# Hybrid decoder trunk (SSD and S5): S5 output and feed-through matrices without their zeros, as 64x64 matmuls on the array's diagonal

## The reference

```python
bu_re = einsum('blgc,gnc->blgn', ug, bbar_re)   # and bu_im
s = associative_scan over l of  s[l] = a * s[l-1] + bu[l]     (complex)
y = einsum('blgn,gcn->blgc', s_re, c_re) - einsum('blgn,gcn->blgc', s_im, c_im)
y = y.reshape(bsz, L, 2048) + d_skip * u
v = gelu(y) @ w_glu
```

## Time and profile before

| | |
|---|---|
| median of 3 runs | 2636.06 us (2634.53 to 2640.14) |
| the profiled execution, its own time | 2637.47 us |
| its span, first to last instruction | 2635.7 us |
| mean granted clock of TensorE | 0.983 |
| PE busy | 2527.9 us (96%) |
| DVE busy | 1684.8 us (64%) |
| ACT busy | 1114.4 us (42%) |

### The profile page before, as it was taken

One profiled execution on the slowest core, in us unless ns is written; L12 is line 12 of the kernel. 1 busy time (PEld: TensorE's weight loads), 2 busy tenths in 40 slices (PEclk: granted clock), 3 DMA queues, 4 the chain that ended last, 5 costly groups with the idle time before them and its releaser, 6 DMA issues.

```text
span 2635.7 us, 53075 instructions
## 1 busy us (share of the span) xinstructions
PE 2527.9 (96%) x19434; PEld 2457.4 (93%) x19434; DVE 1684.8 (64%) x3144; ACT 1114.4 (42%) x1761; POOL 67.4 (3%) x81
## 2 busy tenths in 40 slices
PE   5999999999999999999999999979999999999996
PEld 4989999999999989999999999969999999999996
DVE  4768778786887867668886666574544554544444
ACT  4544535444453534454425333343333443333332
POOL 1000000000000001100000000000000000000000
PEclk9999999999999999999999999989999999999998
DMA  5665657666565668544456776555555555565552
GB/s 149 181 188 171 189 156 213 181 183 191 171 183 170 211 155 232 158 119 135 151 156 199 199 202 188 168 157 165 169 166 163 166 159 166 167 199 166 166 164 73
DMA packets 656789, 450.96 MB, mean 171 GB/s; under 512 B 71160, under 2 KB 647944, under 8 KB 655648
## 3 DMA queue, kind: packets, MB, share of 16 engines
q1 hardware_dynamic: 636480, 433.44, 55.9%
q10 hardware_dynamic: 20128, 15.15, 1.9%
HBM read 409.35 MB, written 39.12 MB: 170 GB/s over the span
## 4 chain that ended last, share of the span: by engine, by line
PE 85%; DVE 9%; issue 3%; ACT 1%; DMA 1%; SPq 0%; ACTq 0%; DVEq 0%
PE acc L1924 26%; PE acc L1925 25%; PE acc L1926 25%; PE side L1911 2%; DVE abc L1322 2%; DVE w_lo L1243 2%; PE side L2241 1%; PE side L2007 1%; PE side L2090 1%; ACT w_hi L773 1%; PE side L2276 1%; PE side L2277 1%; DVE cacc L1286 1%; PE side L2261 1%; PE side L2080 1%
## 5 line engine op out<-in xcount | busy, mean ns | idle before, releaser
L1243 DVE TENSOR_TENSOR w_lo<-raw,w_hi 128x1024 fp32r<-128x1024 f32 (+2 forms) x692 | 846.2, 1228 | 709.3 <-ACT w_hi L773 704.1
L773 ACT ACTIVATE w_hi<-raw 128x1024 fp32r<-128x1024 f32 (+2 forms) x692 | 721.6, 1046 | 1061.8 <-PE acc L1926 1022.8
L1924 PE MATMUL acc<-h_hi,w_hi 128*128 128x288 f32 x3472 | 1056.1, 304 | 14.4 <-DVE w_lo L1243 7.8
L1926 PE MATMUL acc<-h_hi,w_lo 128*128 128x288 f32 x3472 | 1029.8, 297 | 0.0
L1925 PE MATMUL acc<-h_lo,w_hi 128*128 128x288 f32 x3472 | 1028.8, 296 | 0.0
L1924 PEld LDWEIGHTS acc<-h_hi,w_hi 128*128 128x128 f32 x3472 | 659.2, 190 | 33.2 <-issue 24.2
L1925 PEld LDWEIGHTS acc<-h_lo,w_hi 128*128 128x128 f32 x3472 | 658.8, 190 | 0.3
L1926 PEld LDWEIGHTS acc<-h_hi,w_lo 128*128 128x128 f32 x3472 | 657.8, 189 | 0.0
L1924 PE MATMUL acc<-f_hi,w_hi 128*128 128x288 f32 x704 | 208.7, 296 | 0.0
L1926 PE MATMUL acc<-f_hi,w_lo 128*128 128x288 f32 x704 | 207.5, 295 | 0.0
L1925 PE MATMUL acc<-f_lo,w_hi 128*128 128x288 f32 x704 | 207.2, 294 | 0.0
(11 more groups left out here) (345 smaller groups left out, 2898.4 us busy)
## 6 DMA issues: line engine op xcount, KB each, us to landing
raw<-in_w_in_dram SPq DMA_DIRECT2D x512, 256.0 KB, 3.2
raw<-in_w_ffn_up_dram SPq DMA_DIRECT2D x352, 256.0 KB, 3.3
raw<-in_w_ffn_down_dram SPq DMA_DIRECT2D x160, 256.0 KB, 3.0
raw<-in_w_ssm_out_dram SPq DMA_DIRECT2D x128, 256.0 KB, 3.3
raw<-in_w_glu_dram SPq DMA_DIRECT2D x128, 256.0 KB, 3.6
h<-in_state_ssm_dram SPq DMA_DIRECT2D x64, 256.0 KB, 4.2
out_ssm_sample_dram<-h SPq DMA_DIRECT2D x64, 256.0 KB, 2.9
raw<-in_w_out_dram SPq DMA_DIRECT2D x64, 256.0 KB, 3.0
```

What stands on the lines that cost most here:

```text
L773: copy = lambda out, in_, **k: nc.scalar.activation(out, in_, ACT.Copy, **k)
L1243: tt(w_lo[:, slot, 0:n], raw[:, slot, 0:n], w_hi[:, slot, 0:n].bitcast(F32), ALU.subtract).then_inc(lo_ready, 1)
L1924: mm(o_, wh, xh[:, kt, :], start=first and i == 0, stop=False)
L1926: done = mm(o_, wl, xh[:, kt, :], start=False, stop=last and i == n - 1)
```

## The change

The output matrices go into four buffers `obd`, each [128, 2, 8, 64]: the two 64x64 blocks of a pair lie one in the upper and one in the lower 64 partitions, without zeros. They take the memory of `qbd` and `qbd2`. `tbd` is laid out likewise, and its memset goes. Each product becomes two matmuls, one of partitions 0 to 63 into PSUM partitions 0 to 63, one of 64 to 127 into 64 to 127. `o_matrices` and `t_block` write all 128 partitions at once. With four buffers the matrices of blocks 1 to 3 are made at z = 36, 39, 42, 45, 48 and 51, inside the scan, and blocks 4 to 7 after `y_add(i - 4)`.

```diff
-    'tbd_zero': ('dec_raw', 1), 'bbar_ready': ('a_exp', 1), 'u2_landed': ('x_landed', 48),
+    'bbar_ready': ('a_exp', 1), 'u2_landed': ('x_landed', 48),
-    tbd, _ = sb("tbd", [P, 2, PB, P], F32, used["pw5"][0])
+    obd = [sb(f"obd{i}", [P, 2, PB, 64], F32, used["qbd"][0] + 4096 * i)[0] for i in range(4)]
+    tbd, _ = sb("tbd", [P, 2, PB, 64], F32, used["pw5"][0])
-            pool.wait_ge(sem("p_copied"), 32)
-            pool.memset(tbd[:, :, :, :], 0.0).then_inc(sem("tbd_zero"), 1)
...
 def t_block(i):
-                if i == 0:
-                    act.wait_ge(*reach("tbd_zero", 1))
                 wait(act, "t_product", i * 2 - 2)
-                for g2 in range(2):
-                    r = slice(64 * g2, 64 * g2 + 64)
-                    for j in range(DL):
-                        src = gs5[r, i * PB:i * PB + PB, :] if j == 3 else (s2, s3)[i % 2][r, (2 - j) * P:(3 - j) * P].rearrange("p (g c) -> p g c", c=S5C)
-                        last = copy(tbd[r, i % 2, :, 64 * g2 + 16 * j:64 * g2 + 16 * j + 16], src)
+                for j in range(DL):
+                    src = gs5[:, i * PB:i * PB + PB, :] if j == 3 else (s2, s3)[i % 2][:, (2 - j) * P:(3 - j) * P].rearrange("p (g c) -> p g c", c=S5C)
+                    last = copy(tbd[:, i % 2, :, 16 * j:16 * j + 16], src)
...
+                if bd.shape[-1] == 64:
+                    last = tt(bd[:, part, :, :].rearrange("x p (j c) -> x p j c", j=DL), v[0], v[1], op)
+                else:
...
...
 def o_matrices(i, part):
-                if i < 2:
-                    dve.wait_ge(*reach("r_product", 7 + i))
-                    dve.wait_ge(sem("c_ready"), 4)
-                wait(dve, "y5_product", i * 2 - 2)
-                matrices(i, part, (qbd, qbd2)[i % 2], ct5, po5, ALU.add, ALU.subtract, "o")
+                if i < 4:
+                    dve.wait_ge(*reach("r_product", 7 + i // 2))
+                wait(dve, "y5_product", i * 2 - 6)
+                matrices(i, part, obd[i % 4], ct5, po5, ALU.add, ALU.subtract, "o")
 ...
-                if z in (T0 + 12, T0 + 18):
-                    o_matrices(1, (z - T0 - 12) // 6)
+                if SCAN0 + 8 <= z < SCAN0 + 26 and (z - SCAN0 - 8) % 3 == 0:
+                    o_matrices(1 + (z - SCAN0 - 8) // 6, (z - SCAN0 - 8) // 3 % 2)
                 if out_block(z - 1) >= 0:
                     i = out_block(z - 1)
                     y_add(i)
-                    if i + 2 < 8:
-                        o_matrices(i + 2, 0)
-                        o_matrices(i + 2, 1)
+                    if i + 4 < 8:
+                        o_matrices(i + 4, 0)
+                        o_matrices(i + 4, 1)
...
 def t_products(i, h):
                 for p in range(4 * h, 4 * h + 4):
-                    last = mm((s0, s1)[h][:, (p % 4) * NK:(p % 4 + 1) * NK], tbd[:, i % 2, p, :], u2[:, i * PB + p, :], **one)
+                    for r in (0, 64):
+                        last = mm((s0, s1)[h][r:r + 64, (p % 4) * NK:(p % 4 + 1) * NK], tbd[r:r + 64, i % 2, p, :],
+                                  u2[r:r + 64, i * PB + p, :], **one)
...
 def s5_out(i, m):
-                q, banks = (qbd, qbd2)[i % 2], ((s0, s1), (s2, s3))[i % 2]
+                q, banks = obd[i % 4], ((s0, s1), (s2, s3))[i % 2]
                 for p in (2 * m, 2 * m + 1):
-                    mm(v, q[:, 0, p, :], st5[:, :, 0, pair], start=True, stop=False)
-                    last = mm(v, q[:, 1, p, :], st5[:, :, 1, pair], start=False, stop=True)
+                    for k in range(2):
+                        for r in (0, 64):
+                            last = mm(v[r:r + 64, :], q[r:r + 64, k, p, :], st5[r:r + 64, :, k, pair], start=k == 0, stop=k == 1)
```

More of the change, by code:

```diff
@@ L320, in build @@
     assert at <= used["ct5"][1]
-    fo5, at = sb("fo5", [PAIRS, 18, P], F32, used["tbd"][0])
+    fo5, at = sb("fo5", [PAIRS, 18, P], F32, used["pw5"][0])
     assert at <= used["en5"][0]
@@ L1051, in t_block @@
                 act.wait_ge(*reach("t_shifted", i + 1))
-                if i == 0:
-                    act.wait_ge(*reach("tbd_zero", 1))
                 wait(act, "t_product", i * 2 - 2)
-                for g2 in range(2):
-                    r = slice(64 * g2, 64 * g2 + 64)
-                    for j in range(DL):
-                        src = gs5[r, i * PB:i * PB + PB, :] if j == 3 else                             (s2, s3)[i % 2][r, (2 - j) * P:(3 - j) * P].rearrange("p (g c) -> p g c", c=S5C)
-                        last = copy(tbd[r, i % 2, :, 64 * g2 + 16 * j:64 * g2 + 16 * j + 16], src)
+                for j in range(DL):
+                    src = gs5[:, i * PB:i * PB + PB, :] if j == 3 else \
+                        (s2, s3)[i % 2][:, (2 - j) * P:(3 - j) * P].rearrange("p (g c) -> p g c", c=S5C)
+                    last = copy(tbd[:, i % 2, :, 16 * j:16 * j + 16], src)
                 last.then_inc(sem("tbd_ready"), 1)
@@ L1632, in matrices @@
                 dve.wait_ge(*reach(s + "_products", i * 4 + (2 * part + 2)))
[L1633 to L1636, removed]
+                if bd.shape[-1] == 64:
+                    last = tt(bd[:, part, :, :].rearrange("x p (j c) -> x p j c", j=DL), v[0], v[1], op)
+                else:
+                    for g2 in range(2):
+                        r = slice(64 * g2, 64 * g2 + 64)
+                        dst = bd[r, part, :, 64 * g2:64 * g2 + 64].rearrange("x p (j c) -> x p j c", j=DL)
+                        last = tt(dst, v[0][r], v[1][r], op)
                 last.then_inc(sem(s + "_matrices"), 1)
```

## The result

The changed kernel takes 2646.67 us (median of 11 runs, 2643.0 to 2649.6), the kernel before on the same chip 2635.33: a ratio of 1.0041 [1.0032, 1.0051]. The ratio makes 10.8 us, the two medians differ by 11.3. Predicted were 2645.3 and +9.2. The profiled execution took 2644.74 with a span of 2643.0.

What follows compares the result with a forecast made beforehand. PE was taken to bound the kernel, with 85% of the chain. Scan +1.6, clock +2.2 and 32 output bursts +5.4 gave +9.2 us on the profiled 2637.47, or 2645.3 against the median 2636.06; range 2631 to 2655.

Steps and rivals of the forecast that it cites:

- the forecast's own narrower range: Whole kernel: 2641 to 2649 us, with the clock held or not and 0.02 us a burst either way; chance 0.62.
- Output bursts, +5.4: Output stage: each of 32 bursts rises from 1.01 to 1.18 us, +5.4 us in all.
- I take 0.11 for its streaming: Output bursts: streaming 72 columns of `st5`, 512 bytes apart, takes 0.11 us a step, eight steps a burst.
- Change of form, 0.30 a burst: Split bursts: going from whole-array matmuls to halves and back costs 0.30 us, paid once a burst.
- Halves side by side: Split bursts: both halves run at once, so a burst has eight steps, not 16.
- rival 2: Split bursts: halves go one after the other, output bursts add +11 to +34 us, 2653 to 2676 us; chance 0.13.
- Rival 1: Output bursts: 512-byte steps cost little once halves load less, a burst takes 0.82 us, total 2633.8 us; chance 0.19.
- Rival 3: Split bursts: change of form costs less than 0.30 us; at 0, total 2636 us; chance 0.06.
- Feed-through, 0.82: Feed-through: each of 16 bursts falls from 0.90 to 0.82 us, 1.3 us less, lost in the wait for DVE.
- Scan's end, +1.6: Scan on DVE: moved output matrices make its last step 1.6 us later, bounds 0 and 3.
- Clock, +2.2: Behind PE's wait before the first output burst: clock falls to 0.50, costing 2.2 us, bounds 0 and 2.6.
- 17 steps: Main matmuls after that wait: 17 steps at half clock take 4.08 us instead of 2.24.

Runs made afterwards that it cites:

- experiment 3: Changed kernel with the upper half (partitions 64 to 127) of every output product left out; 2654.96 us in one run.
- experiment 2: Kernel before, whole output products streaming contiguous `u2` in place of the states at 512-byte steps; 2631.87 us, ratio 0.9989.
- experiment 1: Changed kernel, half output products streaming contiguous `u2` in place of the states at 512-byte steps; 2632.47 us, ratio 0.9991.
- experiment 11: Kernel before with only the feed-through products as two 64x64 halves, output products left whole; 2632.51 us, ratio 0.9989.
- experiment 4: Changed kernel with the output matrices made on DVE in the order of the kernel before; 2644.52 us, ratio 1.0039.

## Why the prediction was right, and where its terms were off

Right: the direction, the cause and most of the size, 9.2 of 10.8 us, and 2646.67 lies in the forecast's own narrower range too.
- **Output bursts, +5.4: mis-sized.** They cost +0.305 each, +9.8. The step that failed is "I take 0.11 for its streaming": the gap between the first two records of a whole burst was read as the time of the stream. Experiment 3 has 0.125 for a lone half. So the 0.126 a record of the earlier trace rows, which I put down to weight loads that hide the stream, was the strided stream itself, at a pace that holds at either clock (experiment 3); without the stride the record takes 0.112 (experiment 2). 8 x 0.125 + 0.30 = 1.30 would have been right.
- **Change of form, 0.30 a burst: right.** 0.32 to 0.35 by merging. The estimate from 64-column bursts at other places carried over, and it is what makes the contiguous feed-through bursts hardly cheaper.
- **Halves side by side: right**, against rival 2. The halves of a pair start mostly 5 to 9 ns apart, and the second half adds 0.005 us to a burst (1.311 to 1.316). The Trainium skill (TensorEngine Tiling (Array Packing), section "Gotcha 1: PSUM Pressure") has it that different row tiles cannot access one PSUM bank at once; here that does not hold, since the two halves write one bank, in partitions 0 to 63 and 64 to 127, at the same time.
- **Rival 1: wrong**, by experiment 1: the stride stays with the halves in full. Rival 3's price of form is excluded as well.
- **Feed-through, 0.82: nearly right** with 0.846. The first distance of a burst is 0.114, not 0.065. That its gain is lost in the wait is true of the changed kernel, where DVE has little slack, and false of the order before (experiment 11).
- **Scan's end, +1.6: about right.** It came 1.1 us later against the first feed-through record. A part of `o_matrices` cost DVE 1.93 us in the scan (two `w_lo` starts with a part between them at 1209.45 and 1214.89, without one 3.51 apart), for which I had 1.96, and DVE did not idle again, as forecast. The wait was 3.5 and not 4.1.
- **Clock, +2.2: right in kind, too large.** It fell to 0.50, but cost 0.7 us: six main matmuls came at its pace, where I had counted 17 steps. I took the spell behind the wait of 4.0 as a fixed price; it varies at the same place (first shift to first feed-through record: 7.98 us in the changed kernel, 8.85 in experiment 4, whose code up to there is the same) and after the wait of 3.5 us it cost 0.7 here and over 8 in experiment 3.

The output term was 4.4 us too small, those of the scan and the clock together 2.0 too large. As measured the three make 11.6 where the sum had 9.2. The misses partly cancel: that the total is better than its terms is luck.

## What to carry over

Splitting a block-diagonal matmul into halves bought only weight-load time here: compare the time of the stream with the load first, taking it from a run with the operand made contiguous and not from the gap of a burst's first two records. Each stay in the split form costs a fixed amount, so gather the split matmuls; and use it where the moving operand is contiguous. Before work is moved to an engine with idle time, look what that idle time follows: here it tied the scan's end to TensorE, and filling it cut the tie.

## What was not expected of the hardware

A moving operand of 72 fp32 columns takes 0.125 us a record at steps of 64 bytes as at 512, and at most 0.062 contiguous. At steps of 512 bytes it takes no longer at a granted clock of 0.50. On DVE single strided numbers cost 0.41 to 0.43 us for 128x128 in place of 0.29, runs of eight nothing. After the wait of 3.5 us the clock was back at 1.00 by 1308 us, less than 7 us after PE's return, when both halves worked, and only after 1336 us, over 32 after it, when the upper half of the output products was left out; why is not settled by one run.
